# Moving the last hand-over DMAs of SyncE past a block boundary

## The reference, cut to what matters

```python
g = jax.nn.softmax(sc.astype(jnp.float32), axis=-1).astype(xt.dtype)
act = jax.nn.gelu(jnp.einsum('thkd,td->thk', jnp.take(u_tab, eidx, axis=0), xt))
return jnp.einsum('thk,thkd->td', g * act, jnp.take(v_tab, eidx, axis=0))
```

## Time and profile before

| what | us |
|---|---|
| median of 3 runs (lowest, highest) | 3856.0 (3841.12, 3856.24) |
| time of the profiled execution | 3853.9 |
| its span | 3851.8 |
| TensorE busy, whole span | 3547.2 |
| VectorE busy | 3419.5 |
| GpSimd busy | 1958.6 |
| the two handovers to `experts` (first ScalarE instruction) | 863.1 and 2757.2 |
| last matmul of `experts` starts, layer 1 | 1933.3 |

### The profile page before, as it was taken

How to read it: one execution, slowest core, us unless ns; L and a number is a source line. 1 busy time by engine, 2 the same in 40 slices (tenths; PEclk the granted TensorE clock), 3 DMA queues, 4 the chain that set the end, 5 groups by cost and what they waited for, 6 DMA issues and landing times. The chain is left out here.

```text
span 3851.8 us, 60773 instructions
## 1 busy us (share of the span) xinstructions
PE 3547.2 (92%) x20332; PEld 3196.1 (83%) x20352; DVE 3419.5 (89%) x7139; ACT 1416.3 (37%) x2495; POOL 1958.6 (51%) x1568
## 2 busy tenths in 40 slices
PE   4989999589999999999978999958899999999997
PEld 4957799469999999999978678957789999999996
DVE  8975769988999999999989666799799999999998
ACT  3332332473333333333333223317533333333333
POOL 1000123586677677777610002227767777777774
PEclk9988999799999999999989889989999999999998
DMA  6720101259999999999957001103699999999997
GB/s 243 235 72 24 63 23 40 83 215 408 405 405 405 405 395 407 406 405 405 374 181 231 26 1 63 45 18 153 280 405 405 405 405 405 395 406 405 405 405 275
DMA packets 308141, 1033.75 MB, mean 268 GB/s; under 512 B 31354, under 2 KB 83386, under 8 KB 301314
## 3 DMA queue, kind: packets, MB, share of 16 engines
q0 software_dynamic: 147456, 536.94, 35.4%
q1 hardware_dynamic: 160514, 494.71, 33.9%
HBM read 977.45 MB, written 53.56 MB: 268 GB/s over the span
## 5 line engine op out<-in xcount | busy, mean ns | idle before, releaser
L1687 POOL DMA_INDIRECT picked_rows<-in_v_rows,chosen x512 | 801.8, 1566 | 260.4 <-DVE y L2022 141.9
L1687 POOL DMA_INDIRECT picked_rows<-in_u_rows,chosen x512 | 743.2, 1452 | 330.8 <-DVE dots_now L2014 213.3
L1893 PE MATMUL ps<-hd_hi,u_hi 128*128 128x384 f32 x2048 | 698.0, 341 | 1.3 <-DVE a_lo L2004 1.3
L1893 PE MATMUL ps<-hd_hi,u_lo 128*128 128x384 f32 x2048 | 694.1, 339 | 0.0
L1893 PE MATMUL ps<-hd_lo,u_hi 128*128 128x384 f32 x2048 | 693.2, 338 | 0.0
L2022 DVE SCALAR_TENSOR_TENSOR y<-picked_rows,dots_now,y 128x1024 f32<-128x1024 f32 x512 | 643.6, 1277 | 0.1
L2014 DVE CUSTOM_DVE_ANT_0 picked_rows<-picked_rows,h2rows 128x1024 f32<-128x1024 f32 x512 | 615.3, 1216 | 18.5 <-DMA picked_rows<-in_u_rows,chosen 17.0
L1904 PE MATMUL ps<-v_hi,a_lo 128*128 128x512 f32 x1536 | 474.5, 390 | 0.0
L1904 PE MATMUL ps<-v_hi,a_hi 128*128 128x512 f32 x1536 | 473.3, 389 | 0.0
L1904 PE MATMUL ps<-v_lo,a_hi 128*128 128x512 f32 x1536 | 472.9, 389 | 0.0
L1227 POOL TENSOR_TENSOR wout_lo<-wout_even,wout_hi 128x2048 fp32r<-128x2048 f32 x4 | 18.3, 4577 | 773.8 <-ACT wout_hi L1128 773.8
(11 more groups left out here) (324 smaller groups left out, 7133.4 us busy)
## 6 DMA issues: line engine op xcount, KB each, us to landing
u_raw<-in_u SPq DMA_DIRECT2D x256, 512.0 KB, 14.3
v_rest<-in_v SPq DMA_DIRECT2D x192, 512.0 KB, 8.0
mod_ring<-in_ada SPq DMA_DIRECT2D x96, 512.0 KB, 4.4
gt<-gates_dram SPq DMA_DIRECT2D x60, 768.0 KB, 15.4
gates_dram<-gmat SPq DMA_DIRECT2D x10, 4096.0 KB, 11.5
v_first<-in_v SPq DMA_DIRECT2D x64, 512.0 KB, 12.5
wq<-in_wq SPq DMA_DIRECT2D x32, 512.0 KB, 3.5
w_odd<-in_w_in SPq DMA_DIRECT2D x8, 1024.0 KB, 4.9
```

The lines of the kernel that those rows point to most:

```text
L1687: pool.indirect_dma_start(picked_rows[:, n % RING, :], None, a[table], bass.IndirectOffsetOnAxis(ap=chosen[:, m % GT, m // GT:m // GT + 1] ...
L1893: ins = pe.matmul(ps[:, b % 2, 0:TD], (u_hi, u_lo)[wl][:, b % 2, k, :], (hd_hi, hd_lo)[hl][:, k, :], start=(k == 0 and n == 0), stop=(k == ...
```

## The change

SyncE's eight DMAs are shared out anew. In the gate stage only the `gt` load and the `gmat` copy for q = 0 remain (function `first_gates`). V block 0, the store of columns 32 to 80 and the two loads for q = 1 are issued at the start of `experts`, ahead of the wait for `g_part`; the other two stores are issued after V blocks 1 to 3. SyncE's wait for `staged` in the gate stage goes. `g_own` becomes two semaphores; VectorE waits for the second one at block 4 of each body.

```diff
+    def first_gates(sp, q):
+        sp.dma_start(gt[:, q, 0:NB - 1, :, :].rearrange("p b k t -> p b (k t)"),
+                     gates_dram[0:NB - 1, :, 4 * q * GB:4 * (q + 1) * GB].rearrange("b p n -> p b n")
+                     ).then_inc(g_in[q], 16)
+        sp.dma_start(gt[:, q, NB - 1, :, :], gmat[:, 0, 4 * q:4 * q + 4, :]).then_inc(g_own[q], 16)
...
                         sp.wait_ge(gm_stored[0], 16 * turns + 16)
-                        sp.wait_ge(staged, turns + 1)
-                        for q in range(2):
-                            blocks = slice(4 * q, 4 * q + 4)
-                            sp.dma_start(gt[:, q, 0:NB - 1, :, :]..., gates_dram[...]...).then_inc(g_in[q], 16)
-                            sp.dma_start(gt[:, q, NB - 1, :, :], gmat[:, 0, blocks, :]).then_inc(g_own, 16)
-                        sp.dma_start(v_first[:, :], a["v"][l, 0]).then_inc(v_in[0], 16)
-                        for (lo, hi), done in (((32, 80), g_part), ((0, 32), gm_stored[1]), ((80, NKEYS), gm_stored[1])):
-                            sp.dma_start(gates_dram[NB - 1, :, lo * GB:hi * GB],
-                                         gmat[:, 0, lo:hi, :].rearrange("p a b -> p (a b)")).then_inc(done, 16)
+                        first_gates(sp, 0)
                         return
...
+                def last_gates(lo, hi):
+                    return sp.dma_start(gates_dram[NB - 1, :, lo * GB:hi * GB], gmat[:, 0, lo:hi, :].rearrange("p a b -> p (a b)"))
+
+                load_v(0, 0)
+                last_gates(32, 80).then_inc(g_part, 16)
+                first_gates(sp, 1)
                 sp.wait_ge(g_part, 16)
                 for b in range(1, 4):
                     load_v(0, b)
+                last_gates(0, 32).then_inc(gm_stored[1], 16)
+                last_gates(80, NKEYS).then_inc(gm_stored[1], 16)
                 sp.wait_ge(gm_stored[1], 16 * (NB // 2) + 32)
...
-                dve.wait_ge(g_own, 32)
+                dve.wait_ge(g_own[0], 16)
                 def gate(g, b):
                     dve.wait_ge(g_in[b // 4], g * 16 + 16)
+                    if b == 4:
+                        dve.wait_ge(g_own[1], 16)
```

More of the change, by code:

```diff
@@ L1680, in build_program @@
     gm_stored = [K.sem(f"gm_stored{i}") for i in range(2)]
-    g_own = K.sem("g_own")
+    g_own = [K.sem(f"g_own{i}") for i in range(2)]
     g_part = K.sem("g_part")
@@ L1702, in store @@
                         sp.wait_ge(gm_stored[0], 16 * turns + 16)
-                        sp.wait_ge(staged, turns + 1)
-                        for q in range(2):
-                            blocks = slice(4 * q, 4 * q + 4)
-                            sp.dma_start(gt[:, q, 0:NB - 1, :, :].rearrange("p b k t -> p b (k t)"),
-                                         gates_dram[0:NB - 1, :, 4 * q * GB:4 * (q + 1) * GB].rearrange("b p n -> p b n")
-                                         ).then_inc(g_in[q], 16)
-                            sp.dma_start(gt[:, q, NB - 1, :, :], gmat[:, 0, blocks, :]).then_inc(g_own, 16)
-                        sp.dma_start(v_first[:, :], a["v"][l, 0]).then_inc(v_in[0], 16)
-                        for (lo, hi), done in (((32, 80), g_part), ((0, 32), gm_stored[1]), ((80, NKEYS), gm_stored[1])):
-                            sp.dma_start(gates_dram[NB - 1, :, lo * GB:hi * GB],
-                                         gmat[:, 0, lo:hi, :].rearrange("p a b -> p (a b)")).then_inc(done, 16)
+                        first_gates(sp, 0)
                         return
```

## The result

| what | before | after |
|---|---|---|
| median of 5 runs each (lowest, highest), us | 3848.19 (3841.12, 3856.24) | 3878.69 (3875.87, 3904.2) |
| profiled execution: its time, its span | 3853.9, 3851.8 | 3894.9, 3892.7 |
| start of `experts` (first ScalarE instruction), layers 1 and 2 | 863.10, 2757.2 | 869.50, 2784.08 |

The ratio after/before is 1.0085, with a 95% interval of 1.0057 to 1.0113. The change makes the kernel slower, by some 33 us of 3850, and the time lies outside the range that was given. Behind each experiment "Measured" gives the same ratio to the kernel before, from runs of both side by side, with its interval.

What follows compares the result with a forecast made beforehand. It took TensorE to set the pace inside `experts`, with the DMA engines just as full. Hidden 4 later by 2.8 and 3.4 us, less later gaps of 0.8 and 1.5, gave +3.9 us: 3860 us, range 3841 to 3871.

Steps and rivals of the forecast that it cites:

- Mechanism and sign of my sum: Both layers: earlier barrier, but TensorE waits for U block 4 at hidden 4; +3.9 us, slower; chance 0.50.
- The barrier, 3.0 us earlier: End of gate stage: with fewer bytes beside the gathers, the last one lands sooner; `experts` starts 3.0 us earlier each layer.
- The set now ends at 887.2: SyncE's transfers ahead of U block 4, layer 1: same bytes, all landed at 887.2 instead of 885.9, 1.3 us later.
- 0 to 1.8 us: Start of `experts`: gathers running ahead put more bytes in front of the stores; 0 to 1.8 us a layer, range only.
- The wait for `g_part` at nothing: SyncE at the start of `experts`: V blocks 1 to 3 queue behind this wait; the store has less ahead; no cost.
- The landing of U block 4, 5.0 us: After U block 4's issue in `experts`: its 512 KB load beside gathers takes 5.0 us to land.
- The 2.35 us for the split: Between U block 4's landing and hidden 4: the block is split 2.35 us after it is there.
- Given back, 0.8 and 1.5 us: Later gaps of TensorE in `experts`, 0.8 and 1.5 us in the kernel before, go away.
- The clock, up to 2.9 us a layer, not in the sum: TensorE's gap at hidden 4 could lower the granted clock again; 2.9 us a layer, up to +5.8 in all.
- Rival A: Start of `experts`: U block 4 is in time, the earlier start stays; 3.0 to 5.4 us a layer, 3839 to 3850; chance 0.25.
- Rival B: GpSimd's drain is a fixed 9 us after its last issue; barrier stays, DMAs late; +10.1 us, 3866; chance 0.20.
- Rival C: Barrier: SyncE was last to arrive; 6 us a layer gained with no deadline behind, 3844; chance 0.05.

Runs made afterwards that it cites:

- e6: Against the kernel before: gathers 0 to 3 issued at the start of `experts` instead of the gate stage's end; 1.0009 of before.
- e11: e8 with the store of columns 32 to 80 back beside the gathers and the other two behind U blocks 5 and 6; 1.0006 of before.
- e12: e8 with the two last stores spread, one behind U block 5 and one behind U block 6; 1.0011 of before.
- e9: Against the changed kernel: the `gt` load for q = 0 (640 KB) issued ahead of the `gm_taken` wait; 1.0052 of before.
- e7: Against the changed kernel: gathers 8 to 15 fetch 512 bytes of each row instead of 4 KB; 1.0025 of before.
- e4: Against the kernel before: only the two last stores issued behind V blocks 1 to 3, all else left in the gate stage; 1.0031 of before.
- e2: Against the changed kernel: store wait moved to the first `gt` reload, and the two last stores issued behind U block 4; 1.0030 of before.
- e8: Against before: V block 0, `gt` loads before `gm_taken` wait; store 32 to 80 starts `experts`; other stores behind U block 4, their wait at block 3; 0.9971.

## Why the prediction was wrong

Mechanism and sign of my sum held: the barrier is GpSimd's drain, the drain is the last gather's landing (e6, e11, e12), the early start does not last, TensorE waits before hidden 4 on U block 4, whose issue stands behind the stores. The sizes did not. By the prediction's own steps:

- *The barrier, 3.0 us earlier.* It moved 1.3 and 0.1 us in the two layers, 0.5 by the means above. I took the bytes removed at the full rate, 2.1 us, and more on top. What stayed, the `gt` load, was worth 2.1 us (e9), what went about 0.5. In after this load and the fourth gather both land at 868.8, with the DMA share at 0.39 from 867 on: the last microseconds of that landing are not explained by bytes in the queues. What they wait for stays open.
- *The set now ends at 887.2.* This is the step that failed. It puts the stores' landing 38.6 us after the first gather. They landed at 881.0 + 22.0 = 903.0, 46.7 after it, and U block 4 was issued at 47.1 instead of 38.9. The step took the set of bytes ahead of U block 4 as fixed, whatever their order, and so added 1.3 us. But SyncE now waits twice in a row, 9.3 us for A and then 22.8 for B and C, and in that time the gathers go on: up to U block 4's arrival 3.46 MB more came through, at least 2.7 of them gathers, for which I had kept 0 to 1.8 us and left them out of the sum. The rate up to then was 346 GB/s instead of 366. e7 shows that taking such bytes away gives back 4.8 us, e4 that the order alone, with the place of before, costs 15.2, where my step has nothing for it (the same bytes in another order).
- *The wait for `g_part` at nothing.* The first store, A, was issued 13.6 us after the first gather instead of 9.0 and was 9.3 us on the way until SyncE's next DMA, instead of 12.3. It did land quicker, as I had it, but not by as much as it was later: V blocks 1 to 3 went out at 22.9 instead of 21.2. ScalarE waited 2.95 us for V block 1, and none of it reached TensorE.
- *The landing of U block 4, 5.0 us.* 5.2, right. The 2.35 us for the split became 2.90 (908.58 to 911.48).
- *Given back, 0.8 and 1.5 us.* Right.
- *The clock, up to 2.9 us a layer, not in the sum.* It fell, and took 2.5 and 2.6. I left it outside for a gap of 5.8 us; in e2 3.05 us of standing weight loads already cost 1.3, so it belonged inside.
- Rival A (the start stays) falls with the gap. Rival B, a fixed drain, is refuted as a mechanism by e11 and e12, but its condition, "wherever the barrier moves by less than about 1 us", was met in layer 2 and by the means (not by the 1.3 us of layer 1), and its place is the right one; its price of 5.9 us was taken by the same fixed set and is half of the real one. Rival C falls by the drains.

Summed: 11.7 + 12.8 + 2.5 + 2.6 - 0.8 - 1.5 = 27.3 us measured against 2.8 + 3.4 - 0.8 - 1.5 = 3.9 forecast. The chance of 0.07 for slower by over 0.5% rested on the same size: no case came near the 27 us because each took the set as fixed.

## What to carry to other kernels

Where the DMA engines are as full as the engine that sets the pace, a stretch in which they have room (here the 8 us ahead of the last gate matrix) is what is worth filling; moving transfers on into the full part costs, even when it frees the barrier. A block whose issue stands behind a wait for stores is late by whatever the other streams bring in the meantime, so the sum must count those streams for as long as the wait lasts, and not the bytes of one queue. Two waits in a row on one queue add up even when the bytes are the same. Store behind the loads that are due first, and wait where the stored data is read. Before pricing an earlier start, ask whether the first consumers have data: in e6 6.7 us of earlier start were worth nothing, in e8 and e12 3 to 4 us were worth 1.5 to 3.9 by the traces.

## What the runs showed of the hardware that was not expected

- A drain of GpSimd with gathers outstanding lasts until they land (15.0 us, 2.93 without; its end agrees with the last landing to 0.3 us in four kernels, for landings of 6.0 to 10.8 us), and it holds all engines' barrier.
- 640 KB in 1 KB pieces beside four gathers of 4 KB pieces delayed the last gather by 2.1 us, all that the change removed beside them by about 0.5. One store of 1.5 MB issued 3.6 us behind the first gather held the start of `experts` back by 4.4 us (e11 against e12); the stores that the change took out had left only 9 us behind it.
- Fewer bytes did not mean a set that much faster: with 3.67 MB of gather bytes gone (and smaller pieces in their place) the DMA rate over the handover fell from 346 to 298 GB/s. And a wait for 2.6 MB of stores lasted as long as one for 4.2 MB (22.8 and 21.1 us), both with the engines full.
- 14 us without matmuls ended at a granted clock of 0.50, the 1.2 GHz level, and cost 2.5 us behind it; 3.05 us without weight loads cost 1.3 in e2.
- A stage whose work ahead of its end is nearly the same in all kernels ended up to 28 us apart (841.2 to 869.4) in their profiled runs; a difference of two spans says little below that, and a common point inside both traces must be used.
